# The last RMS norm of a two-layer decoder step: weights multiplied in earlier, the root applied in the copies out of PSUM

## The chip, the cores and the metric

The kernel runs on one core of one Trainium2 chip. The metric is the device time of one launch in microseconds. TensorE (PE) multiplies matrices into PSUM, VectorE (DVE) and ScalarE (ACT) work elementwise on SBUF and PSUM, GpSimd (POOL) helps on SBUF, and SyncE (SP) issues most of the DMAs.

## The reference, cut to what matters

Two layers (a sparse-attention layer, then a pooling layer), each followed by a squared-ReLU MLP, run over 1024 prompt rows and 8 x 4 sample rows of 1024 features. The change touches the very end, the norm after the second MLP:

```
def rmsnorm(x, g):
    xf = x.astype(jnp.float32)
    y = xf * lax.rsqrt(jnp.mean(xf * xf, axis=-1, keepdims=True) + RMS_EPS)
    return (y * g.astype(jnp.float32)).astype(x.dtype)

x = x + g2[:, None, :] * sq_relu_mlp(h, w_up[i], w_down[i])     # last residual of layer 1
y = rmsnorm(x, final_norm_g)                                    # y_prompt (1,1024,1024), y_sample (8,4,1024)
```

## The kernel before, in words

The residual stream `x` stays in SBUF, turned: `x[:, k, :]` holds the features 128k to 128k+127 on the partitions and all 1056 rows (1024 of the prompt, 32 of the samples) along the free dimension. The rows are worked on in three chunks of 352 (`CW`), the features in eight tiles (`KT8`). Everything is written as blocks, one instruction stream for each engine, with semaphores written out by hand; at the end of a block all engines meet before the next begins.

`mlp_block(1, ...)` (L2021) is the block before the change. Its eight outer steps run 36 products a step on TensorE; in the last step the down products give, for each feature tile m and chunk c, one PSUM bank. VectorE adds it into x (`residual`, L528; for chunk 2 also L2200) and counts `down_empty`. Behind its own work ScalarE then squares `x[:, m, c]` (L2126 to L2130, `square`, L580): into `acc` for m = 0, into one of four buffers `sq` for m > 0. GpSimd adds the squares to `acc` (`add_squares`, L591). TensorE sums `acc` over the partitions with one-column products (`norm_tensor`, L610), one for each of nine 128-row tiles, so that the mean square of each row lies on the row's partition in PSUM, in bank 0.

The last block (L2422) makes the output in nine tiles of rows (eight of 128, one of 32):

- VectorE computes the reciprocal root of the mean squares in five small operations, with one square root on ScalarE (`norm_diagonals`, L626; `norm_root`, L621). It writes nine diagonal matrices `diag` (L641).
- TensorE multiplies them by ones (`norm_spread`, L644), which spreads the roots of all rows over all partitions, in PSUM (`pair3` and bank 5).
- For each tile of rows VectorE makes `hf = x * gain * root` in eight operations of 128x128 (L2442).
- TensorE turns the tile in eight transposes (L2432) into one of two PSUM pairs, ScalarE copies it into one of two buffers `yrow` (L2454), and SyncE stores it (L2462). TensorE waits for the copy two tiles before, ScalarE for the store two tiles before.

The gains of the last norm are `gains[:, 32:40]`, one column for each feature tile. The load of the modulation weights of layer 1 in earlier blocks (`load_mod1`, L428; `mod1_landed`, L432) counts on one semaphore for each of eight buffers.

Of the kernel before, what the change touches and what calls it, by code (L numbers as in the profile page):

```python
# [7 lines left out]
ALU = mybir.AluOpType  # L8
# [6 lines left out]
D = 1024  # L15
# [15 lines left out]
EPS = 1e-6  # L31
# [112 lines left out]
def hybrid_step(nc, x_prompt, x_sample, cache_k, cache_v, cache_kidx, state_pool, page_table, c_prompt, c_sample,  # L144
# [3 lines left out]
    with ctx:  # L148
# [90 lines left out]
        assert tt2.manual_sbuf_range[1] <= tt.manual_sbuf_range[1]  # L239

        put = region(r1)
        yrow = put("yrow", [P, 2, D])


        put = region(x.manual_sbuf_range[0])
# [64 lines left out]
        def wide(i):  # L310
            return pair[i][:, :, :].rearrange("p a b -> p (a b)")
# [14 lines left out]
        def sem(name):  # L326
            return ctx.enter_context(nc.semaphore(name))
# [23 lines left out]
        kir_in = [sem(f"kir_in{i}") for i in range(2)]  # L351
        ki_upper, ki_rest, q_upper, q_rest = (sem(n) for n in ("ki_upper", "ki_rest", "q_upper", "q_rest"))
        q_moved = [sem(f"q_moved{i}") for i in range(2)]
        mraw1_in = [sem(f"mraw1_in{i}") for i in range(8)]
        x_out, x_in, kts1_done = sem("x_out"), sem("x_in"), sem("kts1_done")
        cand_late, cand_early = sem("cand_late"), sem("cand_early")
        a_counted, v_counted, cnt_zero = sem("a_counted"), sem("v_counted"), sem("cnt_zero")
# [19 lines left out]
        srow_in, band_in, pstate_t, pstate_done = sem("srow_in"), sem("band_in"), sem("pstate_t"), sem("pstate_done")  # L377
        pool_st = sem("pool_st")
        y_t, y_copied = sem("y_t"), sem("y_copied")
        yst = [sem(f"yst{i}") for i in range(2)]  # L380

        counts = {"v": 0, "p": 0}

# [6 lines left out]
        def chain(eng, ins, key, signal):  # L390

            eng.wait_ge(signal, signalled(ins, key, signal))
# [21 lines left out]
        def load_mod_step(sp, n, dst, signal):  # L414
            layer, m = MOD_LIST[n]
            sp.dma_start(dst, w_mod[layer, :, m * 256:(m + 1) * 256].rearrange(
                "(k p) c -> p k c", p=P)).then_inc(signal, 16)
# [9 lines left out]

        def load_mod1(sp, n):  # L428

            load_mod_step(sp, M_FIRST + n, MOD_HOME[MOD_SLOT[n]][:, :, :], mraw1_in[MOD_SLOT[n]])  # L430

        def mod1_landed(pe, n):  # L432
            pe.wait_ge(mraw1_in[MOD_SLOT[n]], 16 * MOD_SLOT[:n + 1].count(MOD_SLOT[n]))
            return MOD_HOME[MOD_SLOT[n]]

        def mod_product(pe, out, weights, ks=range(KT8)):
# [134 lines left out]
        def sq_place(n, d, c):  # L571
            if n not in PHASED:
                return 21 * (n - 1) + 3 * (d - 1) + c
            return 21 * (n - 1) + (2 * (d - 1) + c if c < 2 else 14 + d - 1)
# [5 lines left out]
        def square(act, n, d, c):  # L580

            src = x[:, d, c * CW:(c + 1) * CW]
            if d == 0:
                act.activation(acc[:, c, :], src, ACT.Square).then_inc(acc_first, 1)
                return
            i = sq_place(n, d, c)
            if i >= 4:
                act.wait_ge(sq_used, i - 3)
            act.activation(sq[:, i % 4, :], src, ACT.Square).then_inc(sq_ready, 1)
# [78 lines left out]
        def roots(dve, n, lo, hi):  # L668

            if n in PHASED:  # L670
                done = 6 if hi <= FRONT else TILES + 2
            else:
                done = 4 * ((hi + 511) // 512) if hi <= SEQ else TILES + 1
            dve.wait_ge(root_mm, ROOT0[n] + done)
            return wide(3)[:, lo:hi] if hi <= SEQ else bank(5)[:, lo - SEQ:hi - SEQ]
# [1345 lines left out]
        def mlp_block(layer, u0, g0, gates0):  # L2021
# [14 lines left out]
            with nc.Block() as block:  # L2036
# [37 lines left out]
                @block.scalar  # L2074
                def _(act):
                    def unit(i, k):

                        landed = raw_count(u0 + k)
                        act.wait_ge(raw_in[slot(k)], i * 64 + landed)
                        if k < 2:  # L2080
                            act.wait_ge(down_ready, i * 24 + (g0 - 6 + 6 * k))
                        elif k < 6:
                            done = 5 if k == 2 and isinstance(i, int) and i == 0 else 3 * (k - 1)
                            act.wait_ge(up_ready, i * 12 + (h0 + done))
                        else:
                            act.wait_ge(down_ready, i * 24 + (g0 + 6 * (k - 5)))
                        act.activation(whi[:, slot(k), :], wraw[:, slot(k), :], ACT.Copy).then_inc(hi_ready, 1)  # L2087

                    def hidden(i, p, f, c, first):
                        act.wait_ge(up_ready, i * 12 + (h0 + p + 1))  # L2090
                        if h0 + p >= 3:
                            act.wait_ge(hid_ready, i * 12 + (h0 + p - 2))
                        elif not isinstance(i, int):
                            act.wait_ge(hid_ready, i * 12 + (p - 2))
                        act.activation(relu[:, p % 3, :], up_bank(f, c, first)[:, 0:CW], ACT.Relu).then_inc(up_empty, 1)  # L2095
                        act.wait_ge(up_empty, i * 12 + (h0 + p + 1))
                        act.activation(hidh[:, f, c * CW:(c + 1) * CW], relu[:, p % 3, :],  # L2097
                                       ACT.Square).then_inc(square_done, 1)

                    def steps(i, ahead):  # L2100

                        first = isinstance(i, int) and i == 0
                        behind = {4: 2, 5: 3, 8: 4, 11: 5} if first else {2: 2, 5: 3, 8: 4, 11: 5}
                        for p, (f, c) in enumerate(order_first if first else order):
                            hidden(i, p, f, c, first)
                            if p in behind:
                                unit(i, behind[p])
                        unit(i, 6)
                        unit(i, 7)
                        if ahead:  # L2110
                            unit(i + 1, 0)
                            unit(i + 1, 1)

                    if n_in in PHASED:
                        norm_root(act, n_in, 1)
                        back_scalar(act, layer, 24)
                    else:
                        norm_root(act, n_in)
                        unit(0, 0)
                        unit(0, 1)  # L2120
                        split_rows_scalar(act, n_in, layer, 24)
                    steps(0, True)
                    with act.Fori(1, FB - 1) as i:
                        steps(i, True)
                    steps(FB - 1, False)
                    for m in range(KT8):  # L2126
                        for c in range(NC):

                            act.wait_ge(down_empty, 24 * (FB - 1) + g0 + 3 * m + c + 1)
                            square(act, n_out, m, c)  # L2130

                @block.gpsimd
                def _(pool):
# [285 lines left out]
        mlp_block(1, U_MLP1, G_MLP1, 80)  # L2419


        with nc.Block() as block:  # L2422
            @block.tensor
            def _(pe):
                norm_spread(pe, 4)
                for i in range(TILES + 1):
                    n = P if i < TILES else NS
                    pe.wait_ge(hf_ready, KT8 + i + 1)
                    if i >= 2:
                        pe.wait_ge(y_copied, i - 1)  # L2430
                    for k in range(KT8):
                        ins = pe.transpose(wide(i % 2)[0:n, k * P:(k + 1) * P], hf[:, k, i * P:i * P + n], ident)  # L2432
                    ins.then_inc(y_t, 1)

            @block.vector
            def _(dve):
                norm_diagonals(dve, 4)
                for i in range(TILES + 1):
                    r = slice(i * P, i * P + (P if i < TILES else NS))
                    root = roots(dve, 4, r.start, r.stop)  # L2440
                    for d in range(KT8):
                        ins = dve.scalar_tensor_tensor(out=hf[:, d, r], in0=x[:, d, r], scalar=gains[:, 32 + d:33 + d],  # L2442
                                                       in1=root, op0=ALU.mult, op1=ALU.mult)
                    ins.then_inc(hf_ready, 1)

            @block.scalar
            def _(act):
                norm_root(act, 4)
                for i in range(TILES + 1):
                    n = P if i < TILES else NS  # L2450
                    act.wait_ge(y_t, i + 1)
                    if i >= 2:
                        act.wait_ge(yst[i % 2], 16 * (i // 2))
                    act.activation(yrow[0:n, i % 2, :], wide(i % 2)[0:n, :], ACT.Copy).then_inc(y_copied, 1)  # L2454

            @block.sync
            def _(sp):
                for i in range(TILES + 1):
                    n = P if i < TILES else NS
                    sp.wait_ge(y_copied, i + 1)  # L2460
                    dst = y_prompt[0, i * P:(i + 1) * P, :] if i < TILES else y_sample.rearrange("b t d -> (b t) d")
                    sp.dma_start(dst, yrow[0:n, i % 2, :]).then_inc(yst[i % 2], 16)  # L2462
                sp.wait_ge(yst[0], 16 * 5)
                sp.wait_ge(yst[1], 16 * 4)


def u_in_cols(u):
# [49 lines left out]
```

## Time and profile before

| | |
|---|---|
| median of 3 runs | 2386.09 us (2381.39 to 2388.67) |
| the profiled execution, its own time | 2383.11 us |
| its span in the profile | 2381.4 us |
| PE busy | 2237.2 us, 94% |
| DVE, ACT, POOL busy | 1011.1, 777.1, 633.9 us |
| last block, from its first operation to the end of the span | 2351.65 to 2381.4 us |

The span runs from the first to the last record of the profile. Times in the rows are microseconds from its start. The clock of TensorE (PEclk) is given as a share of 2.4 GHz: 1.00 is 2.4 GHz, 0.50 is 1.2 GHz.

### The profile page before, as it was taken

Reading aid. Unit: us, or ns where it says so; the run is one execution under the profiler, and the core shown is the slowest. Engines: PE = TensorE matmul, PEld = TensorE weight load, DVE = VectorE, ACT = ScalarE, POOL = GpSimd, SP = SyncE. Lnnn points to the kernel's source line nnn. Section 1 sums busy time; section 2 is a strip of 40 time slices with the busy share of each in tenths; the row PEclk is TensorE's granted clock in tenths of the full one; section 3 lists DMA queues with packets and bytes.
Section 4 is the critical chain, followed back from the end, with each engine's and each line's share of the span. In section 5 each row is a group of like instructions: output and inputs, shape, how many; then the busy total and the mean of one; then the engine's idle time right before and its main releaser. Section 6 shows DMA issues by size and latency. Waiting matters only on the chain. (4 is left out here: it accounts for less than half of the span.)

```text
span 2381.4 us, 37312 instructions
## 1 busy us (share of the span) xinstructions
PE 2237.2 (94%) x13854; PEld 2058.8 (86%) x13854; DVE 1011.1 (42%) x2500; ACT 777.1 (33%) x1410; POOL 633.9 (27%) x387
## 2 busy tenths in 40 slices
PE   5998899589989999999999999889999999999997
PEld 4885488345578999999999999878999999999996
DVE  2425788776435433233233233456332332332335
ACT  4204577655534312212212212444112122122123
POOL 4110111257736222222222222441222222222223
PEclk8998999789999999999999999999999999999999
DMA  8454464400033111111111112101111111111111
GB/s 307 133 169 139 143 212 145 141 19 1 1 126 88 45 54 45 44 44 45 52 44 44 44 45 73 35 13 35 52 45 44 44 49 48 44 44 44 49 39 73
DMA packets 208671, 170.31 MB, mean 72 GB/s; under 512 B 14478, under 2 KB 202110, under 8 KB 208566
## 3 DMA queue, kind: packets, MB, share of 16 engines
q1 hardware_dynamic: 201917, 154.64, 20.9%
q10 hardware_dynamic: 4160, 8.65, 1.0%
q0 software_dynamic: 2496, 5.77, 0.9%
q8 instruction: 56, 0.92, 0.2%
q14 instruction: 42, 0.34, 0.0%
HBM read 155.85 MB, written 11.64 MB: 70 GB/s over the span
## 5 line engine op out<-in xcount | busy, mean ns | idle before, releaser
L523 PE MATMUL pair<-hhi,whi 128*128 128x352 f32 x2184 | 717.1, 328 | 33.3 <-DVE hlo L724 8.8
L524 PE MATMUL pair<-hlo,whi 128*128 128x352 f32 x2184 | 705.6, 323 | 0.0
L525 PE MATMUL pair<-hhi,wlo 128*128 128x352 f32 x2184 | 705.4, 323 | 0.0
L2137 POOL TENSOR_TENSOR wlo<-wraw,whi 128x1024 fp32r<-128x1024 f32 x127 | 304.6, 2399 | 1145.9 <-ACT whi L2087 1144.7
L523 PE MATMUL pair<-hidh,whi 128*128 128x352 f32 x1536 | 495.9, 323 | 0.0
L524 PE MATMUL pair<-hidl,whi 128*128 128x352 f32 x1536 | 493.1, 321 | 0.0
L525 PE MATMUL pair<-hidh,wlo 128*128 128x352 f32 x1536 | 492.6, 321 | 0.0
L535 DVE SCALAR_TENSOR_TENSOR x<-pair,mod,x 128x352 f32<-128x352 f32 (+1 forms) x432 | 247.3, 572 | 515.5 <-PE pair L525 514.5
L523 PEld LDWEIGHTS pair<-hhi,whi 128*128 128x128 f32 x2184 | 413.1, 189 | 44.4 <-issue 24.1
L524 PEld LDWEIGHTS pair<-hlo,whi 128*128 128x128 f32 x2184 | 414.1, 190 | 0.4
L525 PEld LDWEIGHTS pair<-hhi,wlo 128*128 128x128 f32 x2184 | 412.6, 189 | 0.5
L2087 ACT ACTIVATE whi<-wraw 128x1024 fp32r<-128x1024 f32 x126 | 132.6, 1053 | 609.6 <-PE pair L525 609.6
L2189 DVE TENSOR_TENSOR squ<-relu 128x352 f32<-128x352 f32 x192 | 101.5, 529 | 496.7 <-ACT relu L2095 496.6
L524 PEld LDWEIGHTS pair<-hidl,whi 128*128 128x128 f32 x1536 | 288.9, 188 | 0.0
L523 PEld LDWEIGHTS pair<-hidh,whi 128*128 128x128 f32 x1536 | 288.7, 188 | 0.0
L525 PEld LDWEIGHTS pair<-hidh,wlo 128*128 128x128 f32 x1536 | 288.1, 188 | 0.0
L2095 ACT ACTIVATE relu<-pair 128x352 f32<-128x352 f32 x192 | 89.0, 464 | 472.0 <-PE pair L525 472.0
L493 POOL TENSOR_TENSOR wlo<-wraw,whi 128x1024 fp32r<-128x1024 f32 x36 | 88.9, 2472 | 280.6 <-ACT whi L489 280.6
L1875 POOL TENSOR_SCALAR ss<-ss,small 128x128 f32<-128x128 f32 (+7 forms) x64 | 118.4, 1853 | 82.3 <-DVE small L1882 81.8
L2193 DVE TENSOR_TENSOR hidl<-squ,hidh 128x352 fp32r<-128x352 f32 x192 | 100.8, 525 | 21.1 <-DVE squ L2189 1.9
L2097 ACT ACTIVATE hidh<-relu 128x352 fp32r<-128x352 f32 x192 | 95.8, 499 | 6.1
L1451 ACT ACTIVATE junk_a<-score,cand 128x1024 f32<-128x1024 f32 (+2 forms) x93 | 83.9, 902 | 42.5 <-DVE cand L1532 30.7
(276 smaller groups left out, 1968.6 us busy)
## 6 DMA issues: line engine op xcount, KB each, us to landing
wraw<-in_w_up_dram SPq DMA_DIRECT2D x64, 512.0 KB, 3.9
wraw<-in_w_down_dram SPq DMA_DIRECT2D x64, 512.0 KB, 3.4
mraw_i<-in_w_mod_dram SPq DMA_DIRECT2D x20, 1024.0 KB, 7.1
mraw_q<-in_w_mod_dram SPq DMA_DIRECT2D x12, 1024.0 KB, 5.1
mraw<-in_w_mod_dram SPq DMA_DIRECT2D x8, 1024.0 KB, 9.1
wraw<-in_dsa_w_in_dram SPq DMA_DIRECT2D x16, 512.0 KB, 6.0
mraw_w<-in_w_mod_dram SPq DMA_DIRECT2D x8, 1024.0 KB, 5.2
wraw<-in_dsa_w_o_dram SPq DMA_DIRECT2D x16, 512.0 KB, 4.0
```

Source lines behind the costliest of these rows:

```text
L493: pool.tensor_tensor(wlo[:, slot, :], wraw[:, slot, :], whi[:, slot, :], ALU.subtract).then_inc(lo_ready, 1)
L523: pe.matmul(out, a, hi[:, kr, r], start=(n == 0), stop=False)
L524: pe.matmul(out, a, lo[:, kr, r], start=False, stop=False)
L525: last = pe.matmul(out, b, hi[:, kr, r], start=False, stop=(n == len(ks) - 1))
L535: ins = dve.scalar_tensor_tensor(out=xs, in0=ps[:, 0:n], scalar=mod[:, layer, gate + d, 0:1], in1=xs, op0=ALU.mult, op1=ALU.add)
L1875: pool.tensor_scalar(ss[:, n % SR, 0:L], ss[:, n % SR, 0:L], small[:, 12 + n % SR:13 + n % SR], None, ALU.mult).then_inc(prob_done, 1)
L2087: act.activation(whi[:, slot(k), :], wraw[:, slot(k), :], ACT.Copy).then_inc(hi_ready, 1)
L2095: act.activation(relu[:, p % 3, :], up_bank(f, c, first)[:, 0:CW], ACT.Relu).then_inc(up_empty, 1)
L2097: act.activation(hidh[:, f, c * CW:(c + 1) * CW], relu[:, p % 3, :], ACT.Square).then_inc(square_done, 1)
L2137: pool.tensor_tensor(wlo[:, slot(k), :], wraw[:, slot(k), :], whi[:, slot(k), :], ALU.subtract).then_inc(lo_ready, 1)
L2189: dve.tensor_tensor(squ[:, p % 3, :], relu[:, p % 3, :], relu[:, p % 3, :], ALU.mult).then_inc(hid_square, 1)
L2193: dve.tensor_tensor(hidl[:, f, c * CW:(c + 1) * CW], squ[:, p % 3, :], hidh[:, f, c * CW:(c + 1) * CW], ALU.subtract).then_inc(hid_ready, 1)
```

## The change

The weights of the last norm are multiplied into x by ScalarE in the MLP block, feature tile by feature tile, behind the squares of each tile. The last block then turns `x` itself. The transposes wait only for these products (`hf_ready`), no longer for the roots. There are no diagonals and no spreading: the reciprocal root of each row, `nz`, lies on the partition of its row in the turned tile, and is the factor of the copy out of PSUM. Even tiles are copied by ScalarE, odd ones by VectorE. The turned tiles use three PSUM pairs (1 to 3) in place of two, `yrow` has four buffers in place of two. The last tile turns the last 128 rows, and only its last 32 are copied and stored. To free semaphores, the loads of the modulation weights count on three semaphores in place of eight, by their number modulo 3.

```
-        yrow = put("yrow", [P, 2, D])
+        yrow = put("yrow", [P, 4, D])
...
-        mraw1_in = [sem(f"mraw1_in{i}") for i in range(8)]
+        mraw1_in = [sem(f"mraw1_in{i}") for i in range(3)]
...
-        yst = [sem(f"yst{i}") for i in range(2)]
+        yst = [sem(f"yst{i}") for i in range(4)]
+        y_scaled = sem("y_scaled")
...
-            load_mod_step(sp, M_FIRST + n, MOD_HOME[MOD_SLOT[n]][:, :, :], mraw1_in[MOD_SLOT[n]])
+            load_mod_step(sp, M_FIRST + n, MOD_HOME[MOD_SLOT[n]][:, :, :], mraw1_in[n % 3])
...
-            pe.wait_ge(mraw1_in[MOD_SLOT[n]], 16 * MOD_SLOT[:n + 1].count(MOD_SLOT[n]))
+            pe.wait_ge(mraw1_in[n % 3], 16 * (n // 3 + 1))
...
                             act.wait_ge(down_empty, 24 * (FB - 1) + g0 + 3 * m + c + 1)
                             square(act, n_out, m, c)
+                        if n_out == 4:
+                            act.wait_ge(sq_ready if m else acc_first, sq_place(n_out, m, 2) + 1 if m else 3 * n_out)
+                            act.activation(x[:, m, :], x[:, m, :], ACT.Copy,
+                                           scale=gains[:, 32 + m:33 + m]).then_inc(hf_ready, 1)
...
+        YR = 4
+        def turned(i):
+            return wide(1 + i % 3)
+        def row_part(i):
+            return slice(0, P) if i < TILES else slice(P - NS, P)
...
             def _(pe):
-                norm_spread(pe, 4)
+                pe.wait_ge(hf_ready, 2 * KT8)
                 for i in range(TILES + 1):
-                    n = P if i < TILES else NS
-                    pe.wait_ge(hf_ready, KT8 + i + 1)
-                    if i >= 2:
-                        pe.wait_ge(y_copied, i - 1)
+                    if i >= 3:
+                        pe.wait_ge((y_copied, y_scaled)[(i - 3) % 2], (i - 3) // 2 + 1)
                     for k in range(KT8):
-                        ins = pe.transpose(wide(i % 2)[0:n, k * P:(k + 1) * P], hf[:, k, i * P:i * P + n], ident)
+                        ins = pe.transpose(turned(i)[:, k * P:(k + 1) * P], x[:, k, ROW0[i]:ROW0[i] + P], ident)
                     ins.then_inc(y_t, 1)
...
             def _(dve):
-                norm_diagonals(dve, 4)
-                for i in range(TILES + 1):
-                    r = slice(i * P, i * P + (P if i < TILES else NS))
-                    root = roots(dve, 4, r.start, r.stop)
-                    for d in range(KT8):
-                        ins = dve.scalar_tensor_tensor(out=hf[:, d, r], in0=x[:, d, r], scalar=gains[:, 32 + d:33 + d],
-                                                       in1=root, op0=ALU.mult, op1=ALU.mult)
-                    ins.then_inc(hf_ready, 1)
+                dve.wait_ge(stat_mm, PART0[4] + 1)
+                chain(dve, dve.tensor_scalar(nv[:], stat(4, slice(0, TILES + 1)), EPS, None, ALU.add), "v", vchain)
+                dve.reciprocal(nr[:], nv[:]).then_inc(nr_ready, 1)
+                dve.wait_ge(ny_ready, PART0[4] + 1)
+                chain(dve, dve.tensor_tensor(nr[:], ny[:], ny[:], ALU.mult), "v", vchain)
+                chain(dve, dve.scalar_tensor_tensor(out=nr[:], in0=nr[:], scalar=-0.5, in1=nv[:], op0=ALU.mult,
+                                                    op1=ALU.mult), "v", vchain)
+                dve.scalar_tensor_tensor(out=nz[:], in0=nr[:], scalar=1.5, in1=ny[:], op0=ALU.add,
+                                         op1=ALU.mult).then_inc(diag_ready, 1)
+                dve.wait_ge(diag_ready, PART0[4] + 1)
+                for i in range(1, TILES + 1, 2):
+                    r = row_part(i)
+                    dve.wait_ge(y_t, i + 1)
+                    if i >= YR:
+                        dve.wait_ge(yst[i % YR], 16 * (i // YR))
+                    dve.tensor_scalar(yrow[r, i % YR, :], turned(i)[r, :], nz[r, i:i + 1], None,
+                                      ALU.mult).then_inc(y_scaled, 1)
...
             def _(act):
                 norm_root(act, 4)
-                for i in range(TILES + 1):
-                    n = P if i < TILES else NS
+                act.wait_ge(diag_ready, PART0[4] + 1)
+                for i in range(0, TILES + 1, 2):
+                    r = row_part(i)
                     act.wait_ge(y_t, i + 1)
-                    if i >= 2:
-                        act.wait_ge(yst[i % 2], 16 * (i // 2))
-                    act.activation(yrow[0:n, i % 2, :], wide(i % 2)[0:n, :], ACT.Copy).then_inc(y_copied, 1)
+                    if i >= YR:
+                        act.wait_ge(yst[i % YR], 16 * (i // YR))
+                    act.activation(yrow[r, i % YR, :], turned(i)[r, :], ACT.Copy,
+                                   scale=nz[r, i:i + 1]).then_inc(y_copied, 1)
...
             def _(sp):
                 for i in range(TILES + 1):
-                    n = P if i < TILES else NS
-                    sp.wait_ge(y_copied, i + 1)
+                    r = row_part(i)
+                    sp.wait_ge((y_copied, y_scaled)[i % 2], i // 2 + 1)
                     dst = y_prompt[0, i * P:(i + 1) * P, :] if i < TILES else y_sample.rearrange("b t d -> (b t) d")
-                    sp.dma_start(dst, yrow[0:n, i % 2, :]).then_inc(yst[i % 2], 16)
-                sp.wait_ge(yst[0], 16 * 5)
-                sp.wait_ge(yst[1], 16 * 4)
+                    sp.dma_start(dst, yrow[r, i % YR, :]).then_inc(yst[i % YR], 16)
+                for i in range(YR):
+                    sp.wait_ge(yst[i], 16 * len(range(i, TILES + 1, YR)))
```

## Rows read from the trace of the kernel before

**Rows 1.** The page's first part: busy us, share of the span, instructions.
```profile
PE 2237.2 (94%) x13854; PEld 2058.8 (86%) x13854; DVE 1011.1 (42%) x2500; ACT 777.1 (33%) x1410; POOL 633.9 (27%) x387
```
**Rows 2.** The chain of waits that ended last: start us, us, what.
```profile
2351.65 0.18 DVE nv L632
...
2352.75 0.18 DVE nz L640
...
2352.95 1.37 DVE diag L641
...
2354.37 2.09 PE pair L650 x8
...
2356.49 15.85 DVE hf L2442 x61
...
2376.73 1.01 ACT yrow L2454
```
**Rows 3.** Timeline, 2348 to 2365 us: start, us, engine, line, operation [idle before].
```profile
2348.66 0.50 ACT L589 ACTIVATE sq<-x 128x352 f32<-128x352 f32 x1 [1.70 <-DVE x L2200]
2349.30 0.92 POOL L599 TENSOR_TENSOR acc<-acc,sq 128x352 f32<-128x352 f32 x1 [1.27 <-ACT sq L589]
...
2350.28 1.05 PE L617 MATMUL pair<-cst,acc 128*128 128x1 f32 x8 [1.36 <-POOL acc L599]
...
2364.89 1.09 PE L2432 MATMUL pair<-cst,hf 128*128 128x128 f32 x8 [0.98 <-DVE hf L2442]
```
**Rows 4.** Timeline at 2327 us, ScalarE and GpSimd: squares and their sums.
```profile
2327.03 1.65 ACT L589 ACTIVATE sq<-x 128x352 f32<-128x352 f32 x4
...
2328.40 2.77 POOL L599 TENSOR_TENSOR acc<-acc,sq 128x352 f32<-128x352 f32 x3
...
2329.31 15.40 POOL L599 TENSOR_TENSOR acc<-acc,sq 128x352 f32<-128x352 f32 x17
```
**Rows 5.** ScalarE's groups by form: count | busy us, mean ns | idle before.
```profile
L703 ACT ACTIVATE hhi<-tt,mod 128x352 fp32r<-128x352 f32 x32 | 18.5, 589 | 17.5 <-DVE tt L695 17.5
L2258 ACT ACTIVATE hf<-tt,mod 128x1024 f32<-128x1024 f32 x8 | 9.1, 1140 | 3.4 <-DVE tt L2392 3.4
L2454 ACT ACTIVATE yrow<-pair 128x1024 f32<-128x1024 f32 x8 | 8.2, 1024 | 15.7 <-PE pair L2432 15.7
```
**Rows 6.** Stretches: us, busy of PE, PEld, DVE, ACT, POOL, PEclk, DMA share, GB/s.
```profile
2349.00:2352.50 3.50, 1.05 (x8) 0.97 (x8) 0.54 (x3) 0.37 (x2) 0.92 (x1) 1.00 0.00 0
2352.50:2359.30 6.80, 4.66 (x21) 4.53 (x22) 4.53 (x15) 0.00 (x0) 0.00 (x0) 0.50 0.00 0
2359.30:2373.00 13.70, 7.33 (x55) 5.68 (x53) 13.70 (x54) 6.92 (x7) 0.00 (x0) 1.00 0.54 222
2373.00:2376.40 3.40, 3.24 (x15) 2.76 (x16) 1.37 (x9) 1.27 (x2) 0.00 (x0) 0.50 0.45 186
```
**Rows 7.** Timeline at 19 us: transposes of one tile at the low clock.
```profile
19.22 1.97 PE L859 MATMUL pair<-cst,xrow 128*128 128x128 f32 x8
```
**Rows 8.** VectorE's groups by form: count | busy us, mean ns | idle before.
```profile
L2382 DVE TENSOR_TENSOR hlo<-pair,hhi 128x1024 fp32r<-128x1024 f32 x8 | 9.8, 1224 | 22.0 <-ACT hhi L2250 22.0
...
L1616 DVE TENSOR_SCALAR score<-score,cand,sgn 128x1024 f32<-128x1024 f32 x1 | 0.8, 794 | 0.0
```
**Rows 9.** DMA issues of the stores: count, KB each, us to landing.
```profile
out_dram<-yrow SPq DMA_DIRECT2D x8, 512.0 KB, 2.6
...
out_dram<-yrow SPq DMA_DIRECT2D x1, 128.0 KB, 3.3
```
**Rows 10.** A stretch early, loads in a row: columns as in rows 6.
```profile
10.00:20.00 10.00, 5.21 (x30) 3.31 (x31) 0.80 (x3) 2.08 (x2) 0.35 (x1) 1.00 1.07 392
```
**Rows 11.** Half a microsecond inside a store, columns as in rows 6.
```profile
2364.00:2364.50 0.50, 0.00 (x0) 0.00 (x0) 0.50 (x3) 0.50 (x1) 0.00 (x0) 1.00 1.01 418
```
**Rows 12.** ScalarE's table loads, by form.
```profile
L624 ACT ACT_TABLE_LOAD x2 | 2.6, 1283 | 6.9 <-issue 6.9
...
L1722 ACT ACT_TABLE_LOAD x1 | 1.3, 1283 | 6.7 <-PEq L1357 6.7
```

## The prediction

> **What bounds the kernel now.** I read the page's first part, the chain of waits, the timeline of the last 35 us, the stretches with their clock, and last the groups by form. TensorE is busy 94% of the span [rows 1], and the change takes nothing from its large products. The question is therefore only what lies behind the last product, and there the chain of waits is the view to trust: it names neither TensorE nor the stores but VectorE [rows 2]. From the last block's first operation (2351.65) to the end (2381.4) 29.75 us pass. The five small root operations end at 2352.93. Then come the diagonals (1.37), half of the spreading (2.09), and 15.85 us plus a little in which VectorE multiplies x by gain and root. TensorE's last two tiles, the last copy and the last store follow. TensorE turned a tile in 1.09 us and had sat 0.98 us idle before it, waiting for VectorE [rows 3]; ScalarE's copy took 1.02 [rows 5]. So tiles came every 2.07 us, VectorE's pace, and all others had slack.
>
> **Before the last block.** The last square ends at 2349.16, the last sum at 2350.22, the one-column products at 2351.33, and the block starts about 0.3 later [rows 2, 3]. None of these is removed. Added are eight multiplications on ScalarE of 128x1056 in SBUF. The trace has no such operation. The nearest is L2258, with a factor-like pointer operand, SBUF to SBUF: 1.14 us for 1024 columns; I take 1.17 for 1056. Below, I bound it by the plain copy of L2454 (1.02) and above by twice that (2.0), since there is a wait for ScalarE's own square before each [rows 5]. Seven of them lie beside the last products. ScalarE's squares follow each other every 0.41 us (four in 1.65) but GpSimd sums only one each 0.91 (17 in 15.40): per feature tile GpSimd needs 2.7 us, ScalarE 1.3 + 1.17 = 2.5. The first multiplication comes before the first square of m = 1, at 2327.1, so that square ends at 2328.85 and GpSimd starts its sums some 0.5 later than at 2328.40 [rows 4]. Its row of sums, which ended at 2344.71, ends at 2345.2, and the last sum starts at 2349.30 only because the last square ends at 2349.16 [rows 3]. The cover holds 4 us: no cost. It is gone when ScalarE isn't free by 2348.66: 2327.1 + 7c + 20 squares in about 8.7 us gives c = 1.8 us. The eighth multiplication follows the last square: 2349.2 + 1.17 = 2350.35, before TensorE's one-column products end (2351.33). Slack 1 us: no cost.
>
> **The start of the block.** VectorE's five operations stay, and nz is there at 2352.93 as before. Its new wait is for its own last operation; behind it are only its copies. TensorE no longer waits for any of this: its eight transposes for tile 0 begin at about 2351.6, with `hf_ready` long at 16. Diagonals (1.37), spreading (2.09 on the path, 18 products in all) and 72 VectorE operations are gone.
>
> **TensorE's pace.** Nine tiles of eight transposes are 1.09 us each at the full clock [rows 3] and 1.97 at 1.2 GHz [rows 7]. The clock is at 1.00 up to 2352.5, falls to 0.50 after TensorE had done only 1.05 us of work in 3.5, stays there for 6.8 us and returns, when TensorE has been busy from 2354.4 on [rows 6]. In the new kernel TensorE has the same idle time before the block, so I expect the fall, but its work begins 2.8 us earlier and has no gap, so I expect a shorter low stretch: from 0 to 6.8 us, I take the middle, 3.4 us. Each microsecond of it costs 1 - 1.09/1.97 = 0.45. Tile 0 is ready at about 2352.85, tile 1 at 2354.8, tile 2 at 2356.4, and from there one each 1.09: tile 8 at 2362.9.
>
> **The copies.** ScalarE takes five with a pointer factor. L703 (a pointer, 352 columns) has 0.589, the square of the same width 0.50 [rows 3, 5]: 0.09 for the pointer, so 1.11 for a copy. VectorE takes four of 128x1024 from PSUM. The trace has no such operation with a factor. L2382 reads PSUM and SBUF at that width, 1.22; L1616, from SBUF alone, 0.79 [rows 8]. I take 1.2, as L2382 reads PSUM too. Each engine has a copy every 2.2 us, so both wait for TensorE, and the wait for the copy three tiles before (2.2 us old by then) is never open. Tile 0 is copied from 2352.97 (nz) to 2354.1, tile 7 to 2363.0, tile 8 to 2364.0.
>
> **The stores.** Before, they came every 2.07 us and landed after 2.6 [rows 9]. Now they come every 1.09, faster than one can be moved: 512 KB at 418 GB/s, the rate inside a store, is 1.26 us [rows 11]. A store then lands 2.6 after its issue or 1.26 after the one before, whichever is later. Tile 2 (issued 2357.6) lands at 2360.2, tile 3 at 2361.5, then 2362.7, 2364.0, 2365.2, and tile 7 at 2366.5, which is 0.9 later than alone. The waits of tiles 4 to 8 for the store four before are met (tile 3's has landed before tile 7 is copied, tile 4's before tile 8). The last store alone would land 3.3 after 2364.0 [rows 9]; with 0.9 of queue 2368.2, and 0.3 more to the end of the span, as before: 2368.5.
>
> **The sum.** 2381.4 - 2368.5 = 12.9 us. By the clock's two ends: with no low stretch the stores bind from tile 0 on (first landing 2356.7, seven more by 1.26, then the last) and the span ends at 2367.6, a gain of 13.8; with 6.8 us low it ends at 2369.5, a gain of 11.9. The other edits are costed at nothing: `yrow` of four buffers lies where the MLP's inputs are dead, and the modulation loads wait for the same loads in the same order, with as many instructions. The instruction streams of all loops stay in their places, too, since what is added stands behind the last loop. The profiled execution took 2383.11, 3.0 below the median, so its successor would take 2370.2; against the median of 2386.09 the forecast is **2373.2 us**.
>
> **Rivals.**
> A: the stores don't overlap. Before, each was issued 2.07 us after the last and lands in 2.6, so no more than half a microsecond of overlap is seen. If each took 2.6 of its own: 2356.7 + 7 x 2.6 + 3.3 + 0.3 = 2378.5, a gain of 2.9: 2383.2. Against it: early on, loads in a row move at 392 GB/s [rows 10]. The Trainium skill (DMA: Bandwidth & Descriptors, Bandwidth) speaks for this rival: it advises transfers of at least 1 MiB to reach three quarters of peak, and gives each a fixed cost of some 2 us; by an estimate from that page a 512 KB store alone would take 3.2 us, and unqueued ones would end the span about where it ended before. A half-way form, 2.0 us a store as in their old spacing, gives 2356.7 + 14 + about 2.1 = 2372.8, a gain of 8.6: 2377.5.
> B: the clock stays at 1.2 GHz through all nine tiles. Then 2351.6 + 9 x 1.97 = 2369.3, copy 1.1, and 3.66 from the end of the last copy to the end of the span [rows 2]: 2374.1, a gain of 7.3: 2378.8. For it: at 2373.0 the clock fell although TensorE had been busy 7.33 of 13.7 us. Against: it returned at 2359.3 when TensorE was busy throughout, and at 2376.4 again [rows 6].
> C: TensorE doesn't start at once in the new block, since its instructions or the last multiplication are late by 2 to 3 us: a gain of about 10, 2376.
> D, on the other side: the copy with a factor needs another table than the square. Then each multiplication has two loads of 1.283 [rows 12], c = 3.74 in place of 1.17, past the 1.8 from which it decides. ScalarE would be 7 x 1.94 = 13.6 us late for the last square, 1.5 more for the last multiplication beyond the slack, and two loads stand around the root: about 17 us lost against 12.9 won, 2390. Against it: ScalarE's 0.37 us busy from 2349.0 to 2352.5 is the rest of a square and the root, with a copy soon after [rows 5, 6], so that these three share a table now. The Trainium skill (ScalarE: Activation LUTs, Table sets) says that cheap functions such as the copy are in every set, which speaks against D as well.
>
> **Chances.** Forecast 0.68 (its own range 2370 to 2376.5); A in full 0.05, half-way 0.08; B 0.09; C 0.07; D 0.03. About 0.3%, 7.2 us, can be told from no change. Faster is the forecast, C, half-way A and most of B: 0.88. Within it are A and the rest of B, 0.08, and slower D with what I haven't thought of, 0.04. The three runs shown spread over 7.3 us, so the median of the new ones may be off by 3 by itself. The range that leaves 2 in 10 out is 2367 to 2380: below it reaches past the gain of 13.8, above it takes in B and half of A.
>
> **What would show it.** `diag`, L650 and `hf` gone from the chain, which then holds TensorE's transposes and the stores. Transposes begin within 0.1 us of `nv`. The first copy starts at nz's end, 1.3 us after the block's start. Copies of 1.11 on ScalarE and 1.2 on VectorE, tiles 1.1 apart after a low stretch of about 3.4 us. Stores landing later the further on, the last after 4 us or more. Multiplications of 1.17 with the last sum still starting at 2349.3 on the old scale. It would be wrong if that last sum moved (ScalarE late), if ScalarE showed table loads, or if stores followed each other by 2 us or more.

## The result, and the profile after

The changed kernel takes **2369.88 us** (median of 5 runs, 2369.18 to 2373.41) against 2386.09 before: a ratio of 0.9936 (95% interval 0.9925 to 0.9947), 15.3 us faster (12.6 to 17.9). Timed again beside the experiments it had a ratio of 0.9942 (0.9927 to 0.9957), 13.8 us. The profiled execution took 2369.18 us, span 2367.5, 13.9 below the span before. The forecast was 2373.2, 12.9 less than before, in a range of 2367 to 2380.

The page's first part, columns as in [rows 1], shows what went: 69 operations of VectorE net, 18 products of TensorE. ScalarE has four more (its eight multiplications, minus four copies that VectorE took over).

```profile
PE 2232.2 (94%) x13836; PEld 2056.8 (87%) x13836; DVE 1001.8 (42%) x2431; ACT 782.0 (33%) x1414; POOL 634.6 (27%) x387
```

The chain that ended last, columns as in [rows 2]. It holds none of VectorE's work any more: transposes, a copy, one store's landing, and the last copy, which had waited for that store.

```profile
2352.28 6.24 PE pair L2445 x40
2358.51 0.02 issue
2358.54 1.12 ACT yrow L2477
2359.66 0.02 issue
2359.68 3.20 DMA out_dram<-yrow
2362.88 0.02 issue
2362.90 0.02 ACTq L2476
2362.91 0.05 issue
2362.96 1.11 ACT yrow L2477
```

The timeline from the last product on, columns as in [rows 3]:

```profile
2348.01 0.32 PE L526 MATMUL pair<-hidh,wlo 128*128 128x352 f32 x1
...
2349.28 0.50 ACT L590 ACTIVATE sq<-x 128x352 f32<-128x352 f32 x1 [1.70 <-DVE x L2206]
2349.81 1.18 ACT L2135 ACTIVATE x<-x,gains 128x1056 f32<-128x1056 f32 x1
2349.92 0.93 POOL L600 TENSOR_TENSOR acc<-acc,sq 128x352 f32<-128x352 f32 x1 [1.27 <-ACT sq L590]
...
2352.27 0.17 DVE L2451 TENSOR_SCALAR nv<-pair 128x9 f32<-128x9 f32 x1 [3.02 <-PEq L2037]
2352.28 9.72 PE L2445 MATMUL pair<-cst,x 128*128 128x128 f32 x72 [0.32 <-PEq L2037]
...
2353.59 1.11 ACT L2477 ACTIVATE yrow<-pair,nz 128x1024 f32<-128x1024 f32 x1 [0.65 <-DVE nz L2457]
...
2354.81 1.28 DVE L2465 TENSOR_SCALAR yrow<-pair,nz 128x1024 f32<-128x1024 f32 x1 [1.26 <-PE pair L2445]
...
2361.68 1.28 DVE L2465 TENSOR_SCALAR yrow<-pair,nz 128x1024 f32<-128x1024 f32 x1 [0.99 <-DMA out_dram<-yrow]
2362.96 1.11 ACT L2477 ACTIVATE yrow<-pair,nz 32x1024 f32<-32x1024 f32 x1 [1.56 <-DMA out_dram<-yrow]
```

Look at three things. TensorE's transposes start 0.01 us after `nv`. The last square and the last sum stand as far from the last product as before (1.27 and 1.91 us), with the eighth multiplication beside them. The last two copies wait for stores: they start 0.6 and 1.0 us after TensorE had made their tiles.

The span is a poor ruler for such a tail: the last product started at 2347.39 before and at 2348.01 here, and in the experiments anywhere from 2346.5 to 2351.5, since the work before the last MLP's down products varies from run to run. Those products themselves don't: from the first of them to the start of the last, 687 us, every profile agrees to 0.01 us, with ScalarE's multiplications beside them (after) or without (before). The rows show one in three of them: count, duration in ns min/median/max, start of the first and of the last in us.

```profile
L523 PE MATMUL pair<-hidh,whi x768: 319/323/326, 1660.5 to 2347.1; 128*128 128x352 f32 x192
```

```profile
L524 PE MATMUL pair<-hidh,whi x768: 320/323/325, 1661.2 to 2347.7; 128*128 128x352 f32 x192
```

So the experiments are compared by their **tail**, from the start of the last product to the end of the span. In the kernel before it is 2381.4 - 2347.4 = 34.0 us:

```profile
2347.39 0.32 PE L525 MATMUL pair<-hidh,wlo 128*128 128x352 f32 x1
...
2360.12 1.03 ACT L2454 ACTIVATE yrow<-pair 128x1024 f32<-128x1024 f32 x1 [7.81 <-PE pair L2432]
```

Here it is 2367.5 - 2348.0 = **19.5 us**, 14.5 less. Half of it lies before the first copy: that came 8.5 us after the block's start (2360.12 - 2351.65, [rows 2]) and comes 1.3 after it now (2353.59 - 2352.27). The other half lies behind: from the first copy to the end 21.3 us have become 13.9, since the tiles, one each 2.07 us before, leave as fast as the stores can take them. The stretches, columns as in [rows 6]:

```profile
2353.70:2357.00 3.30, 3.30 (x17) 3.30 (x16) 1.28 (x1) 1.55 (x2) 0.00 (x0) 0.50 0.39 159
2357.10:2361.90 4.80, 4.80 (x45) 4.66 (x43) 2.78 (x3) 2.69 (x3) 0.00 (x0) 1.00 0.96 392
```

TensorE does its first 1.3 us in the block at 2.4 GHz, then 3.4 us at 1.2, then the rest at 2.4. The DMA engines are full from about 2357 until 2366, 1.5 us before the end; the landings of tiles 3 to 7 lie 1.2 to 1.5 us apart:

```profile
2364.50:2365.00 0.50, 0.00 (x0) 0.00 (x0) 0.00 (x0) 0.00 (x0) 0.00 (x0) 1.00 1.03 418
2365.00:2365.50 0.50, 0.00 (x0) 0.00 (x0) 0.00 (x0) 0.00 (x0) 0.00 (x0) 1.00 1.03 426
2365.50:2366.00 0.50, 0.00 (x0) 0.00 (x0) 0.00 (x0) 0.00 (x0) 0.00 (x0) 1.00 1.08 434
```

### The profile page after: what moved, and what is told of

The parts are those of the page before. It is cut to its first block and busy times, and to the rows that moved or that the text cites. A ratio compares the mean times of both kernels' runs of the same rounds, so it can differ in the third digit from the quotient of the medians.

```text
span 2367.5 us, 37205 instructions
## 1 busy us (share of the span) xinstructions
PE 2232.2 (94%) x13836; PEld 2056.8 (87%) x13836; DVE 1001.8 (42%) x2431; ACT 782.0 (33%) x1414; POOL 634.6 (27%) x387
## 5 line engine op out<-in xcount | busy, mean ns | idle before, releaser
L524 PE MATMUL pair<-hhi,whi 128*128 128x352 f32 x2184 | 716.6, 328 | 33.9 <-DVE hlo L725 8.8
```

Source lines behind the costliest of these rows:

```text
L524: pe.matmul(out, a, hi[:, kr, r], start=(n == 0), stop=False)
```

## The experiments

Theory S: the stores hold the end, each about 1.26 us on full DMA engines. What counts is when the first one starts and that none waits for a buffer. Theory C: the copies or the transposes hold it. All ratios are to the kernel before, with 95% intervals. The expectations of the first four count from the block's first operation (15.2 us in the changed kernel), which comes 4.3 us after the last product's start in all of them. Each tail is that of one profile; the changed kernel's two differ by 0.1 us. By the ratios only two of the variants of the changed kernel stand apart from it, two output buffers (from its first timing; the interval of the second is just touched) and the multiplications late; what is said of the others rests on their tails. Each takes one part out of the whole change, so that their costs overlap and don't add up to the 14.5 us.

| kernel | ratio | tail, us |
|---|---|---|
| before | 1 | 34.0 |
| changed | 0.9936 (0.9925 to 0.9947) | 19.5 |
| changed, again | 0.9942 (0.9927 to 0.9957) | 19.6 |
| one copier | 0.9936 (0.9919 to 0.9952) | 20.0 |
| two output buffers | 0.9965 (0.9953 to 0.9978) | 24.4 |
| half stores | 0.9918 (0.9902 to 0.9935) | 17.2 |
| transposes wait for the root | 0.9943 (0.9927 to 0.996) | 21.8 |
| multiplications late | 0.9987 (0.9976 to 0.9997) | 29.9 |
| before, loads' semaphores alone | 0.9999 (0.9986 to 1.0011) | 32.8 |
| before, four buffers alone | 1.0 (0.999 to 1.0009) | 33.9 |
| norm in two parts | 0.9926 (0.9912 to 0.994) | 17.0 |

**One copier.** ScalarE copies all tiles, and the waits of TensorE and SyncE are for its copies alone (cut to the two loops):

```
-                for i in range(0, TILES + 1, 2):        # scalar
+                for i in range(TILES + 1):
...
-                for i in range(1, TILES + 1, 2):        # vector: its loop of copies is left out
```

> The changed kernel, but ScalarE makes all nine copies and VectorE none. In the changed kernel the stores keep the DMA engines full from the third tile on (1.26 us a store at 418 GB/s), ScalarE's copy takes 1.12 us. Theory S (the stores bind the tail): nine copies in a row of 1.12 still come faster than stores of 1.26, so from the block's first operation to the end of the span 15.2 us become at most 16.2, and the time stays within 1 us of the changed kernel (2370 to 2371). Theory C (the copies bind, and the second engine is what brought the gain): 9 x 1.12 from the root on in place of the even and odd copies side by side puts the last copy 3 us or more later, 18 us or more, 2373 and above.

From the block's start 15.8 us, tail 20.0, 0.5 more; the ratio is the same. ScalarE's timeline: six copies in a row, 1.01 us apart, still faster than the stores.

```profile
2357.17 6.17 ACT L2469 ACTIVATE yrow<-pair,nz 128x1024 f32<-128x1024 f32 x6 [0.59 <-PE pair L2445]
2363.51 1.11 ACT L2469 ACTIVATE yrow<-pair,nz 32x1024 f32<-32x1024 f32 x1 [0.18 <-DMA out_dram<-yrow]
```

Theory C falls for the copies. The second engine, one of the parts that the change names, is worth half a microsecond at most: the last copy starts 0.2 us later after the block's start (10.86 in place of 10.69), and the rest lies in the last store, which landed 3.4 us after its issue in place of 3.1. The times don't tell the two kernels apart.

**Two output buffers** (`YR = 2` in place of 4).

> The changed kernel with two output buffers in place of four. A copy then waits for the store two tiles before. A store lands 2.6 to 3.1 us after its issue, a copy takes 1.12 or 1.28: two tiles for each 3.9 us or so, 1.95 a tile in place of the stores' 1.26. Theory S with landing time as the price of a small ring: the last copy starts at the first copy + 4 x 3.9 = 15.6 in place of 9.4, the tail grows by 6 us, 2376. Rival: the stores are bound by their bytes alone and queued enough with two buffers: under 1.5 us more.

Tail 24.4, 4.9 more, where 6 were expected. The last copy started 15.4 us after the first, as expected (15.6); but then the last store found the engines free and landed after 1.9 us in place of the changed kernel's 3.1. The chain of waits shows the price, copy and landing in turn, 3.83 us for two tiles:

```profile
2359.49 1.13 ACT yrow L2477
2360.62 0.02 issue
2360.63 2.61 DMA out_dram<-yrow
2363.24 0.02 issue
2363.26 0.02 ACTq L2476
2363.28 0.04 issue
2363.32 1.12 ACT yrow L2477
```

**Half stores.** Only columns 0 to 511 of each output row are stored:

```
-                    sp.dma_start(dst, yrow[r, i % YR, :]).then_inc(yst[i % YR], 16)
+                    sp.dma_start(dst[:, 0:512], yrow[r, i % YR, 0:512]).then_inc(yst[i % YR], 16)
```

> The changed kernel, storing only the first 512 of the 1024 columns of y (the second half of both y outputs is left out). A store is then 256 KB, some 0.63 us. Theory S: without the stores the next bound is the transposes with the low clock stretch; the last tile is turned 9.7 us after the block's start, is copied without the 1.0 us wait for a store, and the end comes about 3.3 us after it: the tail is 14.2 in place of 15.2 us, a gain of 1. Theory C (copies or transposes bind, stores are hidden): no change beyond the last store's own, 0.3 us. Rival: stores bind alone and by far: a gain of 4 us or more.

From the block's start 12.9 us, tail 17.2, 2.3 less: more than the 1 expected and less than 4. No copy waits for a store, the last one starts 0.9 us sooner after the block's start (2364.07 - 2354.31 = 9.76 in place of 10.69), and the last store lands 1.7 us after its issue in place of 3.1:

```profile
2354.31 9.72 PE L2445 MATMUL pair<-cst,x 128*128 128x128 f32 x72 [0.33 <-PEq L2037]
...
2364.07 1.11 ACT L2477 ACTIVATE yrow<-pair,nz 32x1024 f32<-32x1024 f32 x1 [0.63 <-PE pair L2445]
```

So the stores do hold the end, but TensorE, whose nine tiles take 9.72 us as in the changed kernel, is the next bound, at most 2.3 us behind. That the last store is itself smaller is in this number.

**The transposes wait for the root.**

```
                 pe.wait_ge(hf_ready, 2 * KT8)
+                pe.wait_ge(diag_ready, PART0[4] + 1)
```

> The changed kernel, but TensorE waits for nz before its first transpose: the head start is undone, all else kept. TensorE starts 1.35 us after the block's start, runs at 1.2 GHz (0.213 us for each transpose) after the longer idle time, tile 0 is ready some 3.1 us after the block's start in place of 1.35 (the root). Theory S: the first store starts 1.8 us later and the whole stream of stores is moved by it: the tail is 17.0 us, 2371.5. Rival (the transposes catch up, since the stores hold the end): under 0.5 us. Rival (the low clock holds all nine tiles): 3 us or more.

From the block's start 17.6 us, tail 21.8, 2.3 more. TensorE starts at 2354.86, 1.42 after `nv`; the first tile is ready 2.0 us later, at the low clock, and the first copy comes 2.1 us later after `nv` than in the changed kernel (3.46 in place of 1.32):

```profile
2353.44 0.17 DVE L2452 TENSOR_SCALAR nv<-pair 128x9 f32<-128x9 f32 x1 [3.03 <-PEq L2037]
...
2354.86 8.56 PE L2446 MATMUL pair<-cst,x 128*128 128x128 f32 x64 [1.74 <-DVE nz L2458]
2356.90 1.12 ACT L2478 ACTIVATE yrow<-pair,nz 128x1024 f32<-128x1024 f32 x1 [2.80 <-PE pair L2446]
```

The delay of the first store is carried through to the end, as theory S has it; the transposes don't catch up. The head start of the change is worth these 2.3 us (17.0 from the block's start were expected). The ratios, 0.9943 and 0.9936, don't show it.

**The multiplications late.** They follow ScalarE's root in the last block:

```
-                        if n_out == 4:                  # in the MLP block: left out
...
                 norm_root(act, 4)
+                act.wait_ge(sq_ready, sq_place(4, KT8 - 1, 2) + 1)
+                for m in range(KT8):
+                    act.activation(x[:, m, :], x[:, m, :], ACT.Copy,
+                                   scale=gains[:, 32 + m:33 + m]).then_inc(hf_ready, 1)
```

> The changed kernel, but ScalarE multiplies the weights in at the start of the last block, after its square root, in place of beside the last products. Eight multiplications follow each other every 1.09 us: 8.8 us on the path. TensorE starts its transposes after them, at the low clock, and the first copy starts about 9.9 us later than in the changed kernel. Theory: what the change buys by laying these beside the products is this whole amount, the tail grows by 9.5 to 10.5 us, to 29 to 30, and the time is 2380. Rival (the stores hold the end, so that part of it is absorbed): under 6 us. Rival (VectorE and GpSimd were slowed by the multiplications beside the products, and it comes back when they are moved): the last product starts over 1 us earlier.

Tail 29.9, 10.4 more. The eight take 8.61 us on the path, and TensorE, idle for 9.55 us before its transposes, runs the first 5.7 us of them at the low clock in place of 3.4:

```profile
2353.21 8.61 ACT L2468 ACTIVATE x<-x,gains 128x1056 f32<-128x1056 f32 x8
...
2361.88 10.86 PE L2440 MATMUL pair<-cst,x 128*128 128x128 f32 x72 [9.55 <-ACT x L2468]
2363.95 1.12 ACT L2476 ACTIVATE yrow<-pair,nz 128x1024 f32<-128x1024 f32 x1 [2.12 <-PE pair L2440]
```

This is the largest of the parts that were taken out one by one: without the cover of the last products, 10.4 of the 14.5 us are gone (10.7 by the two ratios). The other 4.1 hold what was not parted further: the diagonals, the spreading and VectorE's 72 operations that went, and the third PSUM pair. Neither rival held. That the multiplications slowed nothing beside the products is seen from the 687 us of the last MLP's down products, the same with them and without; the last product's place in the span (2348.39) can't tell, since it varies by more.

**The loads' semaphores alone**, on the kernel before (`mraw1_in` as in the change, nothing else).

> The kernel before, with only the edit on the loads of the modulation weights: three semaphores in place of eight, counted by the load's number modulo 3. Theory: same loads in the same order, no wait is longer, no change (ratio 1.000 within its interval). Rival: waits that now hang on earlier loads of other buffers, each up to 7 us: slower by 7 us or more. Rival: waits that end earlier, so that some of the 15 us of the change came from here: a ratio below 0.998.

Ratio 0.9999: no cost and no gain beyond what can be told, some 3 us either way. Its tail is 1.2 us shorter than the kernel's before, though the tail's code is the same; the next section says why.

**Four buffers alone**, on the kernel before (`yrow` and `yst` of four, and the three semaphores).

> The kernel before, with only two parts of the change: four output buffers in place of two, and the three semaphores for the loads. Weights, roots, diagonals and VectorE's 72 operations stay. In the kernel before no copy waited for a store, each tile waits for VectorE (2.07 us a tile). Theory: larger rings bring nothing by themselves, 34.0 us from the last product to the end of the span as before, ratio 1.000 within its interval. Rival (the buffers are part of the gain on their own): 1 us or more less.

Ratio 1.0, tail 33.9. ScalarE waits for the transposes as before, 16.2 us in nine times. Yet two buffers in the changed kernel cost 4.9 us: the buffers are worth something only since the tiles come faster.

**The changed kernel again**, in the same group as the one that follows.

> The changed kernel as it is, timed again beside the others of this group: 2370 us, ratio to the kernel before 0.9936, and 19.5 us from the start of the last product to the end of the span (34.0 in the kernel before).

Ratio 0.9942, tail 19.6, as expected. The median was 2373.4 in place of 2370, within the ratio's interval.

**The norm in two parts.** The last block is merged into the MLP block, and tiles 0 to 4, whose rows lie in the first two chunks, get their mean squares, root, transposes and copies first:

```
+            y_stat(pe, 0)                       # tiles 0 to 4
+            pe.wait_ge(hf_ready, 2 * KT8)
+            pe.wait_ge(down_empty, G_MLP1 + 24 * FB - 1)
+            for i in range(2):
+                y_turn(pe, i)
+            pe.wait_ge(down_empty, G_MLP1 + 24 * FB)
+            y_turn(pe, 2)
+            pe.wait_ge(nr_ready, PA + 1)
+            y_stat(pe, 1)                       # tiles 5 to 8
...
+            if n_out == 4 and m == KT8 - 1 and c == 1:   # weights, columns 0 to 703; the other 352 after copy 0
...
+                act.activation(x[:, m, 0:FRONT], x[:, m, 0:FRONT], ACT.Copy,
+                               scale=gains[:, 32 + m:33 + m]).then_inc(hf_ready, 1)
```

> A version built on theory S (the stores hold the end, so what counts is when the first of them starts): the last norm in two parts. The last block is merged into the MLP block. The mean squares of row tiles 0 to 4 are taken once the second chunk of the last feature tile is summed, before the third chunk is ready; their root, their transposes and their copies follow at once; the weights of the last feature tile are multiplied in two parts (704 and 352 columns); tiles 5 to 8 get their root between the copies. By the durations measured, the first copy starts some 2.5 us earlier relative to the last product, and the stream of stores, 10.4 us, with it: 17.0 in place of 19.5 us from the last product to the end, 2367.5. Rival: the gaps between the first stores grow by as much (TensorE turns tiles and makes the second part's sums in turn), so that the end moves by less than 1 us. Rival: VectorE's and ScalarE's waits for the second root hold later copies: slower than the changed kernel.

Tail 2368.4 - 2351.4 = 17.0, as expected. The first copy starts 3.35 us after the last product in place of 5.58:

```profile
2351.39 0.32 PE L526 MATMUL pair<-hidh,wlo 128*128 128x352 f32 x1
...
2352.78 2.82 PE L2050 MATMUL pair<-cst,x 128*128 128x128 f32 x24
...
2354.74 1.11 ACT L2100 ACTIVATE yrow<-pair,nz 128x1024 f32<-128x1024 f32 x1 [1.15 <-PE pair L2050]
```

Its ratio is 0.9926 (0.9912 to 0.994), against 0.9942 for the changed kernel in the same group. The two intervals overlap, so that it beats the changed kernel is seen in the tail (17.0 against 19.5 and 19.6, one profile against two), not shown by the times.

## Why the prediction was right, step by step

**The bound.** VectorE's chain was the bound; it went, and nothing of it came back.

**Before the last block.** A multiplication took 1.18 us (1.17 taken). The last square came 1.27 us after the last product's start, as before, and the products beside them kept their 687 us. The cost of nothing held, and its cover, taken away, was worth 10.4 us.

**The start of the block.** First copy 1.32 us after the block's start, as forecast (1.37). TensorE began at once (rival C fell).

**TensorE's pace: one term that was mis-sized.** I took 1.09 us a tile at the full clock and 1.97 at the low one. These rows were of eight transposes that stood alone, and hold the last one's own time (0.27) besides the seven distances. In a row TensorE's transposes start every 0.109 us, 0.87 a tile (the stretch of 4.80 us above touches 45 of them); at the low clock every 0.213, 1.7 a tile (27 touched in 5.70, in the experiment with late multiplications):

```profile
2361.90:2367.60 5.70, 5.70 (x27) 5.70 (x28) 1.28 (x1) 1.42 (x2) 0.00 (x0) 0.50 0.22 92
```

So the nine tiles took 9.72 us, not the 11.3 of the sum. The low stretch was 3.4 us, the middle that was taken between 0 and 6.8; that it was hit so closely is luck, since no row of the kernel before gave it for this place.

**The copies.** 1.11 on ScalarE (1.11 taken), 1.28 on VectorE (1.2). The waits of tiles 7 and 8 for a store were said to be met; since the tiles came faster than forecast, they were not: the copies started 0.6 and 1.0 us after TensorE had made the tiles. The DMA engines were full meanwhile, so that the waits can have cost little; no run took them away alone.

**The stores: the other term that was mis-sized.** Their rate held, 418 to 434 GB/s; rival A fell. By the sum the span would end 16.9 us after the block's start, and it ended after 15.2. Some 0.7 of this is TensorE's pace (tile 2 was issued 5.3 us after the block's start, not 6.0). The other 1 us is the last store. I took its 3.3 us from [rows 9] as what it takes alone, plus 0.9 of queue; it landed 3.1 after its issue, queue and all, so that the sign "the last after 4 us or more" didn't come. The sum had left its own rule there: a store lands its own moving time behind the one before, and a quarter of the bytes is 0.3 us; tile 7's landed at 2366.8 (3.8 after its issue) and the last at 2367.2. And the 3.3 was not that of a store alone. In the kernel before it had been disturbed. The DMA view of its last microseconds (from 2377.9) has an instruction load, one packet of 16 KB that took 0.93 us from 2378.93 on, beside the stores' packets:

```profile
q1 hardware_dynamic: 102, 0.29, 28.3%
q8 instruction: 1, 0.02, 1.7%
```

In the experiment with the loads' semaphores alone the same code ran without such a packet at that place. The last store landed after 1.9, and the one before it after 2.6 in place of 3.2:

```profile
out_dram<-yrow SPq DMA_DIRECT2D x8, 512.0 KB, 2.6
out_dram<-yrow SPq DMA_DIRECT2D x1, 128.0 KB, 1.9
```

With that goes its tail, 1.2 us shorter, and about as much of the changed kernel's gain in tail is the absence of this load, which the change doesn't promise in every run: it is in the profiles of the kernel before and of the four buffers (landing 3.3 and 3.1), and in neither of the changed kernel's. Three profiles of the same tail agree in this; no run put such a load there on purpose. Against the undisturbed tail of 32.8 the changed kernel's is 13.3 us shorter.

**The sum.** 12.9 forecast, 13.9 between the profiled spans, 14.5 between the tails, 15.3 by the ratio. The two timings of the changed kernel (15.3 and 13.8) lie on either side of the tails' 14.5, and what the ratio has beyond them lies within its interval. The two mis-sized terms erred the same way, so that they didn't cancel: the mechanism was right, and the way from the block's start to the end was forecast 1.7 us too long. Rival B fell too (the clock came back after 3.4 us), as did D: the eight multiplications carry no table load, and the trace has the same loads as before, three of them in [rows 12], none of them here.

## What to carry to other kernels

When a stage of many short steps becomes a stream, time its units in a row: a row of the profile that shows one group standing alone holds the last one's drain, and overstates the pace (1.09 against 0.87 us here). Ask first which resource the stream ends in; here it was the stores, so the second copying engine brought 0.5 us at most, but everything that moved the first store (the head start, 2.3 us; the norm in two parts, 2.5) came through in full in the profiles. And the largest part of the gain was work that was hidden: eight multiplications, 8.6 us in a row when nothing covers them, laid beside products that ran anyway, 10.4 us.

## What the runs showed of the hardware that was not expected

A tensor_scalar of VectorE from PSUM with a pointer factor, 128x1024, takes 1.28 us, more than a tensor_tensor from PSUM and SBUF of the same size (1.22, [rows 8]).

VectorE's small sum of 128x32 in SBUF (L2206) takes 0.19 us alone, and up to 1.65 us beside GpSimd's row of additions. In the kernel with two buffers it started at 2345.35 and ended at 2347.00, as that row did (2346.95):

```profile
2345.35 1.65 DVE L2206 TENSOR_TENSOR x<-x,small 128x32 f32<-128x32 f32 x1
```

```profile
2344.15 2.80 POOL L600 TENSOR_TENSOR acc<-acc,sq 128x352 f32<-128x352 f32 x3
```

The same is seen in the kernel before (0.87 at 2331.26). TensorE's products kept their pace beside it (the same 687 us). That GpSimd was what held it is inferred from the two ends that coincide; no run took GpSimd's additions away.

In the kernel in two parts, where TensorE is never idle for more than 0.34 us between the last product and its last transpose (in the changed kernel 1.37 and 0.32 before the first), the clock stays at 2.4 GHz through all nine tiles, where the changed kernel had its 3.4 us at 1.2 GHz. What this alone brings isn't parted from that of the earlier start.
